# A two-layer decoder trunk on one Trainium2 core: the first stage in another order, attention of the first tile over its own half of the keys, x turned before it is normed, and the stage loop unrolled

## What is computed

```
h = rmsnorm(x) @ w_in                      # queries, keys, values of 3 branches, gates, conv and pool inputs
mixer = [attention over compressed, selected and window keys (8 heads, 2 kv heads of 64),
         gated conv of width 31, pool mixer]
x += mixer @ w_out
x += softmax(rmsnorm(x) @ wq . k_mem) @ v_mem @ wo        # cross-attention, 256 memory tokens, 4 heads
q = rmsnorm(x) @ peer_wq                   # 8 heads x 2 halves of 128
per head: top 16 of 128 in each half, top 16 of the 256 sums -> 16 experts, gates = softmax
x += sum over the 128 experts of a token: gate * gelu(h . u_e) * v_e      # one row of u and of v each
```

## Time and profile before

| | us |
|---|---|
| three runs | 1895.86, 1901.41, 1905.76 |
| median | 1901.41 |
| the profiled execution | 1897.98 |
| its span | 1896.2 |
| busy: PE, VectorE, ScalarE, GpSimd | 1375.9, 1133.7, 514.9, 677.6 |
| DMA: bytes, mean rate | 702.57 MB, 371 GB/s |
| first row gather issued | 243.97 |

### The profile page before, as it was taken

One profiled execution on the slowest core, in us unless ns is written; L12 is line 12 of the kernel. 1 busy time (PEld: TensorE's weight loads), 2 busy tenths in 40 slices (PEclk: granted clock), 3 DMA queues, 4 the chain that ended last, 5 costly groups with the idle time before them and its releaser, 6 DMA issues. The chain is left out here.

```text
span 1896.2 us, 23075 instructions
## 1 busy us (share of the span) xinstructions
PE 1375.9 (73%) x8428; PEld 714.3 (38%) x8428; DVE 1133.7 (60%) x2788; ACT 514.9 (27%) x1311; POOL 677.6 (36%) x1028
## 2 busy tenths in 40 slices
PE   6899956767889983946878863957878874555554
PEld 4666752234554551412444631422444631111110
DVE  5431359876342477689743567688743579864444
ACT  3331122154221222223522222223522221211111
POOL 0000025433333352534433351434433354555551
PEclk9899978889899996977989895977989887777776
DMA  7434589998999999999999998999999999999996
GB/s 272 178 151 178 199 355 399 423 422 353 364 364 399 371 422 409 371 422 403 421 415 397 395 420 346 379 422 400 421 413 397 390 421 371 404 423 421 421 421 268
DMA packets 87380, 702.57 MB, mean 371 GB/s; under 512 B 9952, under 2 KB 10080, under 8 KB 12128
## 3 DMA queue, kind: packets, MB, share of 16 engines
q0 software_dynamic: 73728, 536.90, 68.9%
q1 hardware_dynamic: 13536, 164.15, 21.9%
HBM read 698.92 MB, written 2.10 MB: 370 GB/s over the span
## 5 line engine op out<-in xcount | busy, mean ns | idle before, releaser
L1154 PE MATMUL acc_pe<-uv_rows,diag 64*64 64x512 f32 x4096 | 622.1, 741 | 346.4 <-ACT diag L908 338.0
L461 DVE CUSTOM_DVE_ANT_0 uv_rows<-uv_rows,h_ps 128x1024 f32<-128x1024 f32 x512 | 603.0, 1218 | 196.4 <-DMA uv_rows<-uv_in,idx 191.5
L426 POOL TENSOR_TENSOR diag<-ident_st,gate 128x64 f32<-128x64 f32 x512 | 167.4, 327 | 1097.5 <-PE acc_pe L1154 832.9
L429 POOL DMA_INDIRECT uv_rows<-uv_in,idx x512 | 510.1, 996 | 84.3 <-issue 51.2
L1154 PEld LDWEIGHTS acc_pe<-uv_rows,diag 64*64 64x64 f32 x4096 | 160.3, 158 | 726.6 <-ACT diag L908 501.1
L902 ACT ACTIVATE gelu_b<-act_b 128x2 f32<-128x2 f32 x256 | 51.9, 203 | 901.5 <-DVE act_b L461 891.1
L1181 PE MATMUL bank<-h_t,w_ring 128*128 128x128 f32 x1792 | 210.5, 279 | 11.3 <-DMA w_ring<-blocks_in 9.1
L1181 PEld LDWEIGHTS bank<-h_t,w_ring 128*128 128x128 f32 x1792 | 205.8, 195 | 31.8 <-issue 29.0
L1181 PE MATMUL bank<-w_ring,h_t 128*128 128x512 f32 x448 | 201.0, 603 | 3.0 <-ACTq L944 3.0
L908 ACT ACTIVATE diag<-diag,gelu_b 128x64 f32<-128x64 f32 x512 | 150.2, 340 | 8.4
L1181 PEld LDWEIGHTS bank<-w_ring,h_t 128*128 128x128 f32 x448 | 84.2, 193 | 119.5 <-issue 115.6
(11 more groups left out here) (200 smaller groups left out, 1173.9 us busy)
## 6 DMA issues: line engine op xcount, KB each, us to landing
w_ring<-blocks_in SPq DMA_DIRECT2D x72, 2048.0 KB
uv_rows<-uv_in,idx POOLq DMA_INDIRECT x512
tcon<-tile_consts_in SPq DMA_DIRECT2D x4, 656.5 KB, 13.0
smalls<-smalls_in SPq DMA_DIRECT2D x3, 816.5 KB, 8.5
h_ffn<-ffn_gain_in SPq DMA_DIRECT2D x4, 512.0 KB
xs<-x_in SPq DMA_DIRECT2D x2, 512.0 KB, 10.6
uv_rows<-mem_in SPq DMA_DIRECT2D x1, 1024.0 KB, 16.3
mem_gained<-uv_rows SPq DMA_DIRECT2D x1, 1024.0 KB, 4.8
```

The lines of the kernel that those rows point to most:

```text
L426: nc.gpsimd.tensor_tensor(diag[:, slot_of(k), :], ident_st[:, :], gate[:, k:k + 1].to_broadcast([P, HT]), ALU.mult).then_inc(sems["gates_s ...
L429: nc.gpsimd.indirect_dma_start(uv_rows[:, slot_of(k), :, :].rearrange("p a n -> p (a n)"), None, a["uv"], bass.IndirectOffsetOnAxis(ap=idx ...
L461: v.tensor_tensor_reduce(u_row, u_row, h_ps[:, :], 1.0, 0.0, ALU.mult, ALU.add, act_b[:, k // B % AHEAD, k % B:k % B + 1]).then_inc(sems[" ...
L1154: mm = pe.matmul(acc_pe[c * HT:(c + 1) * HT, r * BLK:(r + 1) * BLK], diag[tok, slot_of(k), :], uv_rows[tok, slot_of(k), 1, c * BLK:(c + 1) ...
```

## The change

1. **Early blocks.** zq, ab and zk1 of the first stage load into slots 4 to 9 of `uv_rows` (two slots a block), zq in two halves with a semaphore each. The order of SP's loads is now: x (first tile), ident, the gain of the first norm, zq, `fixed`, `pos`, ab, mem, the rest of smalls, zk1, tile constants, then zk2 and mk0 into the ring, x (second tile), the gain. The ring then takes ck, cv, mk1, wo0, wo1, mv0, xq0, ...
2. **Order.** FIRST_PLAN is written anew: zq comes before ab, its product takes h_t half by half (`first_rows`); the mem turns are a step of their own; the sine part of the rope tables stands apart; mem products stand between other steps (mem_kv4 and mem_kv5 around xa_norm); one keep_warm of 4 multiplications is left. In all plans the exponentials (`sel_exps`, `win_exps`) and `sel_values` are steps of their own, of length 0.
3. **Own half.** In stages whose dense tile is tile 0 (the first and the third) scores, exponentials, turns and values of sel and win take only keys 0 to 127: two jobs of four heads, one chunk of keys.
4. **Raw x turned.** At the inner norms (xa, ffn) PE turns x itself when the two sums are in it; 1/rms is applied later: in the scale of the cross-attention exponential, in the copy of the half scores, and in h_ffn. x_n and its copy on ScalarE fall away there.
5. **First head alone.** In the first stage pq0, its sub-scores and its ranking are split: the first head's two halves go through PQ0, PK0, rank, pairs and look_up; the second head's as `..._later`. Ten gathers start when the first head is looked up; the gates are spread after them.
6. **Unrolled.** `nc.Fori` becomes a Python `for`; tile addresses are constants, and smalls are loaded only where the tile is 0, so no more in the fourth stage.

```diff
+FIRST_PLAN = ["mix_norm", "rope_tables", "zq", "mem_norm", "rope_sin", "ab", "conv_in", "zk1", "conv0", "mem_turn",
+              "zk2", "conv1", "mem_gain", "mem_kv0", "rope", "turn_kv", "cmp_in", "branch_gates", "mem_kv1", "conv2",
+              "cmp_hidden", "sel_scores", "cmp_hidden_turn", "sel_exps", "mem_kv2", "conv3", "cmp_kv", "sel_turn",
+              "conv_norm", "cmp_scores", "win_scores", "win_exps", "mem_kv3", "cmp_probs", "conv_act", "sel_values",
+              "cmp_out", "win_turn", "sel_out", "conv_silu", "win_out", "small_branches", "mix_turn", "wo0", "wo1",
+              "mem_kv4", "xa_norm", "mem_kv5", "xq0", "xq1", "xa_scores", "mem_kv6", "xa_turn", "mem_kv7", "xa_out",
+              "xo0", "xo1", "keep_warm", "ffn_norm", "pq0", "sub_scores0", "rank0", "rank_pairs0", "look_up0",
+              "pq0_later", "pq1", "sub_scores0_later", "rank0_later", "rank_pairs0_later", "look_up0_later", "pq2",
+              "gates0", "sub_scores1", "pq3", "sub_scores2", "sub_scores3"]
...
+            own_half = dense is not None and tile == 0
+            step_jobs = {**STEP_JOBS, **(TILE0_JOBS if own_half else {}), **(FIRST_JOBS if first else {})}
+            jobs = [job for name in plan for job in step_jobs.get(name, ())]
+            early = EARLY if first else []
+            blocks = [b for job in jobs for b in JOB_BLOCKS.get(job, ()) if b not in early]
...
+            if first:
+                last_use["pq0"] = "PQL"
+            score_jobs, score_heads, keys, key_chunks = (2, 4, P, 1) if own_half else (4, 2, S, 2)
...
+                    at_slot = EARLY_SLOT + 2 * early.index(name)
+                    return uv_rows[:, at_slot:at_slot + 2, :, :].rearrange("p s a n -> p (s a n)").rearrange(
+                        "p (c n) -> p c n", c=KC)
...
+                        n_first = SMALL["gmix"][1]
+                        load_smalls(0, n_first).then_inc(sems["mix_gain_loaded"], 16)
+                        sp.dma_start(early_rows(0, 1), block_of("zq", 0, 2 * D)).then_inc(sems["zq_half_loaded"], 16)
+                        sp.dma_start(early_rows(1, 1), block_of("zq", 2 * D, 2 * D)).then_inc(sems["zq_loaded"], 16)
+                        sp.dma_start(fixed[:, :], a["fixed"]).then_inc(sems["fixed_loaded"], 16)
+                        sp.dma_start(pos[:, :], a["positions"]).then_inc(sems["fixed_loaded"], 16)
+                        sp.dma_start(early_rows(2, 2), block_of("ab")).then_inc(sems["ab_loaded"], 16)
+                        sp.dma_start(mem_raw, a["mem"]).then_inc(sems["mem_loaded"], 16)
+                        load_smalls(n_first, N_SMALL).then_inc(sems["smalls_loaded"], 16)
+                        sp.dma_start(early_rows(4, 2), block_of("zk1")).then_inc(sems["zk1_loaded"], 16)
+                        load_tile_consts()
...
+                    if first:
+                        pool.wait_ge(sems["first_routed"], 1)
+                        pool.wait_ge(sems["mem_g_kept"], 16)
+                        for k in range(ROWS):
+                            gather(k)
+                        pool.wait_ge(sems["gates_ready"], 1)
+                        for k in range(ROWS):
+                            spread_gate(k)
+                        pool.wait_ge(sems["gates_spread"], ROWS)
...
+                        gain_rows(["NX0", "NX1"], "gxa")
                         norm_tail()
-                        gain_rows(["NX0", "NX1"], "gxa")
+                        dve.wait_ge(sems["norm_rstd"], norms[0])
+                        step(v.tensor_scalar(st[:, 28:29], st[:, 3:4], (D // XH) ** -0.5, None, ALU.mult))
...
+                        gain_rows(["NF0", "NF1"], "gffn")
                         norm_tail()
                         dve.wait_ge(sems["ffn_gain_loaded"], 16)
-                        dve.wait_ge(sems["x_normed"], norms[0])
-                        gain_rows(["NF0", "NF1"], "gffn")
-                        v.tensor_tensor(h_ffn[:, :], x_n, h_ffn[:, :], ALU.mult).then_inc(sems["h_scaled"], 1)
+                        dve.wait_ge(sems["norm_rstd"], norms[0])
+                        step(v.scalar_tensor_tensor(out=h_ffn[:, :], in0=xs[:, tile * D:(tile + 1) * D],
+                                                    scalar=st[:, 3:4], in1=h_ffn[:, :], op0=ALU.mult, op1=ALU.mult))
...
+                    def tile_rstd():
+                        norms[0] += 1
+                        s.activation(x_n, xs[:, tile * D:(tile + 1) * D], ACT.Square, accum_out=st[:, 0:1]).then_inc(
+                            sems["norm_squares"], 1)
+                        act.wait_ge(sems["norm_var"], norms[0])
+                        s.activation(st[:, 2:3], st[:, 1:2], ACT.Sqrt).then_inc(sems["norm_std"], 1)
...
+                    def queries(job, lo, n):
+                        copy_bank(pq_t[:, lo:lo + n, :], job, "pq_ready", cols=n * P, view=c_t(n))
+                    def sub_scores(job, lo, n):
+                        if lo == 0:
+                            act.wait_ge(sems["norm_rstd"], norms[0])
+                        copy_bank(half_s[:, lo:lo + n, :], job, "pk_ready", cols=n * P, view=c_t(n),
+                                  scale=st[:, 3:4])
...
+                    def first_rows():
+                        out, w = open_job("ZQ"), weights("zq")
+                        for c in range(KC):
+                            if c % 4 == 0:
+                                pe.wait_ge(sems["zq_loaded" if c else "zq_half_loaded"], 16)
+                                wait_drained(pe, f"NT{c // 4}")
+                            mm = pe.matmul(out[:, :], h_t[:, c, :], w[:, c, :], start=(c == 0), stop=(c == KC - 1))
+                        close_job(mm, "ZQ")
...
+                    def x_turned(jobs2, added):
+                        pe.wait_ge(sems[added], 2)
+                        for i, job in enumerate(jobs2):
+                            at_x = tile * D + i * BLK
+                            turn(job, [xs[:, at_x + c * P:at_x + (c + 1) * P] for c in range(4)])
...
-                        for _ in range(16):
+                        for _ in range(4):
...
+                        if own_half:
+                            outs = [open_job(f"{prefix}{i}") for i in range(2)]
+                            for k in range(4):
+                                for i in range(2):
+                                    h = 4 * i + k
+                                    mm = product(outs[i][:, k * P:(k + 1) * P],
+                                                 [(q_t[head_rows(h), k, :], kv_t[head_rows(h), kind, 0:P])])
+                                    if k == 3:
+                                        close_job(mm, f"{prefix}{i}")
+                            return
...
+                        steps["pq0"] = lambda: cols_product("PQ0", need_weights("pq0"), range(0, 2))
+                        steps["pq0_later"] = lambda: cols_product("PQL", need_weights("pq0"), range(2, 4))
+                        steps["sub_scores0"] = lambda: sub_scores("PK0", 0, 2, 1)
+                        steps["sub_scores0_later"] = lambda: sub_scores("PKL", 2, 2, 2)
...
-        with nc.Fori(1, STAGES - 1) as s:
+        for s in range(1, STAGES - 1):
```

More of the change, by code:

```diff
@@ L100 @@
 BANKS = 4
+EARLY = ["zq", "ab", "zk1"]
+EARLY_SLOT = 4
 PLAN = ["rank1", "rank_pairs1", "look_up1", "gates1", "rank2", "mix_norm", "zq", "ab", "rank_pairs2", "gates2",
@@ L121 @@
             "pq3", "sub_scores3"]
-FIRST_PLAN = ["mix_norm", "rope_tables", "ab", "conv_in", "zq", "mem_norm", "conv0", "zk1", "conv1", "mem_gain",
-              "zk2", "rope", "turn_kv", "cmp_in", "branch_gates", "cmp_hidden", "cmp_hidden_turn", "cmp_kv",
-              "sel_scores", "conv2", "mem_kv0", "sel_turn", "mem_kv1", "conv3", "cmp_scores", "conv_norm",
-              "mem_kv2", "cmp_probs", "mem_kv3", "win_scores", "mem_kv4", "cmp_out", "conv_act", "sel_out",
-              "win_turn", "mem_kv5", "conv_silu", "win_out", "small_branches", "mix_turn", "wo0", "wo1",
-              "keep_warm_xa", "xa_norm", "xq0", "xq1", "xa_scores", "mem_kv6", "xa_turn", "mem_kv7", "xa_out", "xo0",
-              "xo1", "keep_warm_ffn", "ffn_norm", "pq0", "sub_scores0", "rank0", "rank_pairs0", "look_up0", "pq1",
-              "gates0", "pq2", "sub_scores1", "pq3", "sub_scores2", "sub_scores3"]
+FIRST_PLAN = ["mix_norm", "rope_tables", "zq", "mem_norm", "rope_sin", "ab", "conv_in", "zk1", "conv0", "mem_turn",
[7 more added lines that the diff above has]
+              "gates0", "sub_scores1", "pq3", "sub_scores2", "sub_scores3"]
 LAST_PLAN = ["rank1", "rank_pairs1", "gates1", "look_up1", "rank2", "rank_pairs2", "gates2", "look_up2", "rank3",
@@ L299, in stage @@
             last_use = {b: LAST_USE[b] for b in blocks}
-            loads_smalls = dense is not None and (first or mem_layer is None)
+            if first:
+                last_use["pq0"] = "PQL"
+            score_jobs, score_heads, keys, key_chunks = (2, 4, P, 1) if own_half else (4, 2, S, 2)
+            loads_smalls = own_half
```

(9 more changed lines are left out.)

286 lines of the change are left out of this document (157 added, 129 removed), and 4 rows, old and new, of the table STEP_JOBS.

## The result

The changed kernel took 1889.67 us (median of 5 runs, 1887.59 to 1890.11) beside 1900.24 us for the kernel before (5 runs): a ratio of 0.9943, 95% interval [0.9923, 0.9963]. It is faster by 10.6 us (10.8 by the ratio), where 24 were forecast; the sign was right and the size less than half. The time itself, forecast as 1877, lies inside the prediction's own range of 1860 to 1890, at its upper end. The profiled execution took 1887.76 us with a span of 1885.9.

What follows compares the result with a forecast made beforehand. A chain through PE bounds the first stage, the DMA engines bound from 258 us on. Gains of 4 (first stage), 6 (tail), 8 (norms) and 6 (loop) sum to 24 us: 1897.98 becomes 1874, 1877 as median; range 1860 to 1890.

Steps and rivals of the forecast that it cites:

- norms, later stages: Inner norms of later stages: PE no longer waits for root and scaling, gain 8 us, bounds 3 and 10.
- norms, first stage (5 + 3): First stage: norm waits removed, 5.0 us between WO1 and XQ0 and 3.0 between XW1 and PQ0.
- halves: First stage: win scores, a turn and a value product, each twice, fall to half, 7.7 us less; third stage 0.
- loop: Back edge to the fourth stage: unrolling spares all engines a late start, gain 6 us, bounds 3 and 7.
- earlier gathers, tail: First stage's end: first gather about 12 us earlier, stage end as before; gain 6 us, bounds 0 and 12.
- exponentials: Score exponentials behind ScalarE's expert batch: probabilities' turn up to 4 us later, covered by PE's batch work; 0, bounds ±3.
- rest of the first stage, stalls in it: First stage up to PQ0 apart from norms and halves: a loss of 11.7 us, stalls included.
- First stage up to PQ0: First stage until the queries' product: PQ0 at 212 for 216.37, gain 4 us, between -5 and +25.
- three stalls: PE idle in the first stage: 9 us at conv_in, 7.5 for block cv, 5.5 for mk1.
- the stream takes it back: Rival, stages 2 to 4: saved waits reappear as later holes, only 10 us gained, about 1891; chance 0.16.
- The rival of the clock: Rival, first stage: PE's clock stays at 0.50 from 43 to 105 us, 33 us more, 1910; chance 0.04.
- Fillers work: Rival, first stage: its stalls are short or absent, 10 to 21 us better, 1856 to 1867; chance 0.22.

Runs made afterwards that it cites:

- x_normed_turn: The changed kernel with the normalized x turned again instead of raw x, one more ScalarE scaling ahead of the turn: ratio 1.0104.
- x_best_all_keys: The changed kernel with exponentials first, the wait for x's second half and the memory products moved, and tile 0's window attention over all 256 keys again: ratio 0.9775.
- b_unrolled: The kernel before with only the loop over the middle stages written out: ratio 0.9957.
- x_late_gathers: The changed kernel with the first stage's row gathers held until the gates are ready: ratio 0.9923.
- x_pad_scalar: The changed kernel with 24 more wait instructions, on a semaphore already there, at ScalarE's very start: ratio 0.9918.
- x_pad_tensor: The changed kernel with 80 more wait instructions, on a semaphore already there, on TensorE ahead of its first product: ratio 0.9906.
- x_exps_first: The changed kernel with the exponentials of sel and win scores put back ahead of the expert batch on ScalarE: ratio 0.9851.
- x_later_moved: The changed kernel with VectorE's wait for x's second half moved behind conv_in, conv0, conv1 and memory gain, to the norm that needs it: ratio 0.9874.
- x_ring_order: The changed kernel with first-stage memory products moved: mem_kv1 behind mem_kv0, mem_kv2 behind the window's exponentials, mem_kv3 behind the window's turn: ratio 0.9879.
- b_exps_late: The kernel before with only the exponentials of sel and win scores moved behind the expert batch on ScalarE: ratio 1.0126.

## Why the prediction was wrong in size

| term | forecast, us | measured, us, and by what |
|---|---|---|
| norms, later stages | -8 | -24 (x_normed_turn, stages 2 to 4) |
| norms, first stage (5 + 3) | -8 | -13 at PQ0 (x_normed_turn), too much against before |
| halves | -7.7 | -6.5 (x_best_all_keys) |
| loop | -6 | -8 (b_unrolled) |
| earlier gathers, tail | -6 | 0, uncertain by 6 (x_late_gathers to x_pad_scalar) |
| new stall in the tail | none | +5 to +7 (x_pad_scalar, x_pad_tensor) |
| exponentials | 0 | +17.5 (x_exps_first; +14.2 by its stages behind the first) |
| rest of the first stage, stalls in it | +11.7 | some +17, what is left |
| sum | -24 | -10.8 |

The last row but one is a difference, not measured: the sum closes by it. Another reading comes near it: PQ0 is 3.4 us later than before, with 12.6 won by the norms and 7.5 by the halves, so the rest cost 23.5 up to there, and the tail without the stall is 5.3 us shorter than before's 41.9: +18.

**The step that failed most: the exponentials behind the batch, priced at 0 with bounds of 3.** I let the turn of the probabilities come up to 4 us later and covered it by TensorE's work on the batch. The cover is the thing that waits: the batch on ScalarE hangs on VectorE's dot products, and these on VectorE's own queue. The bounds came from no row. The record of before had the size: in its second stage ScalarE waits 185 us for such products, in 41 waits of up to 10.7 us. What the runs showed in place of the 0 is 14 to 24 us: 17.5 when it was undone in after, 23.9 when it was done alone in before.

**Norms of the later stages: mechanism right, term mis-sized.** I priced 8 us by the missing bytes in two windows. The stages followed TensorE's waits, 31.4 us in three stages of before, more than the holes right behind them. That a wait in an in-order chain delays every later slot release is the likely reason, argued and not tested. Holes are only half of it in stages 3 and 4: of the 15.1 us by which stages 3 and 4 of x_normed_turn are longer than after's, 7.9 are idle time of the DMA engines, and in the other 7.2 the packets took longer for the same bytes within 0.5 MB, which no run explains. This error hid the first by luck: 16 us too little gain here, 17.5 too little loss there.

**First stage up to PQ0: right in kind, 7.8 us off.** All three stalls came where and nearly as long as said. WO0 came at 132.36 for 126, 2.8 us of it from the lengths of two stalls, the rest from products that ran at the low clock behind them (mem_kv2 8.77 and mem_kv3 9.07 us for 7.1). Of the runs with the same order of the first stage, x_exps_first had WO0 at 127.78 and a granted clock of 0.95 for 0.92 over the stage, the five others at 130.36 to 132.45. Beside the third stall SP issued a store of 1 MB (`mem_gained`, at 86.54), which the prediction left out. From WO0 to PQ0 it took 87.5 us for the forecast 86. Undoing the norms moved PQ0 by 12.6 us where I had counted 8, but x_normed_turn stands idle where before ran 16 multiplications of ident, and its PQ0 came at the low clock (6.70 us for 3.81); so a part of the 12.6 was no gain on before, and the last row but one of the table takes it up. I called the stalls a cost of 21 us and left it at that. Two edits of a few lines returned 25.

**Tail: wrong.** The gathers came 16.4 us after PQ0 (15.6 forecast), but the stage ended by a stall that no row of before shows, and the first slot came free 0.8 us later, not 10 earlier. The tail without the stall, 36.6 us, was better than the 41 forecast, since pq3's block was hardly late: no gap for it stands ahead of PQ3.

**Loop and halves: right**, 8.2 for 6, and 7.5 us at PQ0 for 7.7. That the halves do nothing in the third stage was right too.

**Rivals.** The rival by which the stream takes it back named 1891, close to the time measured, by a mechanism that did not happen: stages 3 and 4 kept all they won. The rival of the clock did not happen in its size: 0.92 over the stage, and some 3.6 us of longer products. "Fillers work" did not happen in this order of steps; x_later_moved and x_ring_order, which take most of the stalls away, show what it described.

## What to carry to other kernels

Before a step is moved behind other work on an in-order engine, read what that work itself waits for: its waits, not its busy time, are what the step inherits. A wait on the chain that frees the stream's slots cost nearer to its own length here than to the hole in the DMA share behind it. And where a prediction finds stalls that an order of loads or waits makes, they are the next edit: here a wait moved to the step that needs it, and one product moved ahead with two moved back, brought 25 us, more than the change as a whole.

## What the hardware showed unexpectedly

While GpSimd issued ten indirect gathers in a row (one every 1.27 us), TensorE issued a product only every 0.7 to 1.4 us and ScalarE started a copy 6 us late, both until 2 to 3 us after the last gather. VectorE's ranking went on until a step needed ScalarE (5.57 us idle at 252.82). It hangs on where instructions stand on ScalarE and TensorE, as 24 or 80 added waits show, but not by count alone, and it is gone with six gathers in a row. An edit that moves instructions can so gain or lose 5 to 7 us without a cause of its own: the halves in after nearly were judged by it.

The same bytes can take the DMA engines longer. The four kernels that turn the normalized x (before, b_unrolled, b_exps_late, x_normed_turn) have 1723 to 1729 us of packet time in their profiled execution, the fourteen that turn raw x 1711 to 1717. The first three move 0.9 MB more, about 2 us; x_normed_turn moves the same 701.7 MB as after and took 1723.0 us for 1712.8. Why is open.
